# Low halves of every second gate and query tile by an adding DMA transfer; six query tiles from plain fp32 to three split products

## The chip, the cores and the metric

The kernel runs on one core of a Trainium2 chip. The metric is the device time of one execution in microseconds (us). TensorE (PE) multiplies, VectorE (DVE), ScalarE (ACT) and GpSimd (POOL) work on tiles in SBUF, and SyncE (SP) issues most of the DMA transfers; GpSimd issues a few on a queue of its own. Each engine runs its instructions in the order in which they are written and waits on semaphores.

## The reference

One inference step of a one-layer trunk for 256 prompt and 32 sample tokens, so 288 columns, with a model width of 2048. What matters here is its beginning: an RMS norm, one combined input projection, and its three uses.

```python
xn = rmsnorm(h, norm_mix_g)
proj = xn @ w_in                       # 2048 -> 2*1024 (conv) + 1024 (q) + 256 (k) + 256 (v)
a = proj[..., :2 * D_CONV]
glu = a[..., :D_CONV] * jax.nn.sigmoid(a[..., D_CONV:])
xin = concatenate([hist, glu]); y = depthwise_conv(xin, dw_w, width 31)   # then layer norm, silu
new_conv = xin[:, -(CONV_WIDTH - 1):]  # an output: the last 30 columns
q, k = partial_rope(...), partial_rope(...)
h = h + concatenate([conv_out, sliding_window_attention(q, k, v)]) @ w_out
h = h + cross_attention(rmsnorm(h), mem_k, mem_v)     # mem_k, mem_v from mem_prompt
h = h + peer_ffn(rmsnorm(h))                          # 16384 experts, product keys
```

The outputs are compared in fp32.

## The kernel before

**Layout.** Activations lie transposed, 128 rows of the width on the partitions and the 288 tokens as columns. A weight tile is 128 output rows by the whole width: `raw[:, s]`, 128 x 2048 fp32, 1 MB, from DRAM. Four of them (`RAW = 4`) are in SBUF; SyncE loads tile n once tile n - 4 is used (`slot_used`). The first 28 tiles of `w_mix` are the input projection: 16 **gate tiles** (0 to 15, in pairs: even ones give the gate, odd ones the value; 8 pairs for 8 channel tiles), then 12 **query tiles** (16 to 27: four for v and k, eight for q).

**Split products.** TensorE takes fp32 in a plain, slow form, or as fp32r in a fast form with fewer bits. A gate tile is made exact enough by splitting: ScalarE copies `raw` to a high half `wh` (L558), VectorE subtracts, `wl = raw - wh` (L955), and TensorE adds wh x xh, wh x xl and wl x xh for each of the 16 blocks (L1622 to L1624), so 48 matmuls of 288 columns. Both halves are made two tiles ahead (`AHEAD = 2`). The query tiles are not split: 16 plain fp32 matmuls `raw` x `xg` each (L1689). The trace has each of them as two records.

**VectorE between the tiles.** It multiplies the gate (L1037), then the value (L1043, L1044) into `glu`, moves query tiles out of PSUM (L1060, L1063) with the rotary embedding of earlier ones (`VKQ_TURN`, `VKQ_ROPE`: which tile is followed by which rotation), and works through the convolution: 8 channel tiles of 32 steps each (31 taps and a closing step, L1013, L1015, L1003, L1004). How many steps follow each tile is a table: `GLU_CONV` for the gate tiles, `VKQ_CONV` for the query tiles. ScalarE takes the sigmoid of a gate (L596); GpSimd multiplies it by the norm's factor (L2057).

**Memory operands.** After tile 19's load SyncE issues `memT` (4 x 0.5 MB) and `memr` (2 x 1 MB), which ScalarE scales (L607) and squares (L611), and then goes on with tiles 20 to 27. There `memr` and `memT` lie over `wh`, which the query tiles don't use. GpSimd writes out `new_conv` (L2061, L2062), zeroes `kz` and adds up `y` for the layer norm (L2070) as VectorE finishes channel tiles.

## Time and profile before

| | us |
|---|---|
| median of 3 runs | 1980.35 (1979.26 to 1983.44) |
| profiled execution | 1978.63 |
| its span in the trace | 1976.5 |
| gate tiles (from the start) | 0 to 128.3 |
| query tiles | 128.3 to 225 |
| attention with the memory tiles | 225 to 330 |
| the rest: output, cross attention, experts | 330 to 1976.5 |

Times in the rows are us from the span's start. In a timeline the square bracket is how long the engine had been idle before the instruction and what ended that. Matmul records overlap (they are pipelined), so the spacing of their starts tells what one costs, not their length.

### The profile page before, as it was taken

The page shows a single profiled execution, that of the slowest core. Times are in us where ns is not written, and L with a number is a line of the kernel's source. Part 1 is how long each engine was busy: PE and PEld are TensorE (multiplying, and loading weights), DVE is VectorE, ACT ScalarE, POOL GpSimd, SP SyncE. Part 2 cuts the span into 40 slices and gives each one's busy share as a digit, 9 for nine tenths or more (in the row PEclk, how much of TensorE's full clock was granted, in tenths as well). Part 3 has the DMA queues.
Part 4 walks back from the last instruction along what each step waited for, and adds up shares of the span by engine and source line. Part 5 has one row for each costly group of instructions (what it writes and reads, how often), then busy time and mean ns, then how long its engine had stood idle before and what let it go on. Part 6 is the DMA issues. An engine that isn't in the chain of part 4 may idle for free.

```text
span 1976.5 us, 29279 instructions
## 1 busy us (share of the span) xinstructions
PE 1941.4 (98%) x11100; PEld 1743.2 (88%) x11100; DVE 1534.6 (78%) x2297; ACT 857.9 (43%) x869; POOL 701.7 (36%) x497
## 2 busy tenths in 40 slices
PE   6999999999999999999999999999999999999998
PEld 6997888999999999999999999988888888888886
DVE  5999865566788898898888996677777767777776
ACT  4241145445435545555454545534433343344333
POOL 2010110221346778888767872010100011212310
PEclk9999999999999999999999999999999999999999
DMA  5465594444445788878778998899888999999984
GB/s 207 160 198 186 176 397 168 170 150 145 137 147 189 249 290 284 293 269 287 276 282 278 330 336 298 291 337 354 324 338 326 348 334 353 361 341 354 373 317 142
DMA packets 102523, 533.39 MB, mean 270 GB/s; under 512 B 20448, under 2 KB 22656, under 8 KB 46832
## 3 DMA queue, kind: packets, MB, share of 16 engines
q1 hardware_dynamic: 72880, 411.15, 58.0%
q0 software_dynamic: 24272, 106.33, 14.8%
q10 hardware_dynamic: 5296, 14.98, 1.9%
q8 instruction: 39, 0.64, 0.1%
q14 instruction: 36, 0.29, 0.0%
HBM read 493.53 MB, written 38.14 MB: 269 GB/s over the span
## 4 chain that ended last, share of the span: by engine, by line
PE 91%; DVE 4%; ACT 2%; DMA 1%; issue 1%; POOL 0%; DVEq 0%; SPq 0%; ACTq 0%; POOLq 0%
PE acc L1645 20%; PE mis L2024 17%; PE acc L2024 17%; PE acc L1646 10%; PE acc L1622 5%; PE acc L1624 5%; PE acc L1623 5%; PE acc L1689 5%; PE acc L1766 2%; DVE wl L955 1%; DMA raw<-in_u 1%; ACT wh L558 1%; PE mis L1746 1%; DVE xhl L963 0%; DMA hT<-in_xT 0%
## 5 line engine op out<-in xcount | busy, mean ns | idle before, releaser
L955 DVE TENSOR_TENSOR wl<-raw,wh 128x2048 fp32r<-128x2048 f32 x310 | 711.9, 2298 | 273.0 <-ACT wh L558 272.5
L558 ACT ACTIVATE wh<-raw 128x2048 fp32r<-128x2048 f32 x310 | 593.1, 1915 | 578.7 <-DMA raw<-in_v 410.3
L1645 PE MATMUL acc<-xhl,wh 128*128 128x448 f32 x2048 | 643.4, 375 | 1.6 <-DVE wl L955 1.6
L1646 PE MATMUL acc<-xhl,wl 128*128 128x224 f32 x2048 | 540.7, 264 | 0.0
L1645 PEld LDWEIGHTS acc<-xhl,wh 128*128 128x128 f32 x2048 | 384.1, 188 | 32.5 <-DVE wl L955 3.0
L1646 PEld LDWEIGHTS acc<-xhl,wl 128*128 128x128 f32 x2048 | 390.7, 191 | 0.0
L2185 POOL DMA_INDIRECT G<-gsum,cell x224 | 347.8, 1553 | 79.3 <-issue 67.4
L1622 PE MATMUL acc<-xhl,wh 128*128 128x288 f32 x736 | 220.4, 299 | 15.7 <-DVE wl L991 14.1
L1623 PE MATMUL acc<-xhl,wh 128*128 128x288 f32 x736 | 217.7, 296 | 0.0
L1624 PE MATMUL acc<-xhl,wl 128*128 128x288 f32 x736 | 217.4, 295 | 0.0
L2141 POOL DMA_INDIRECT ring<-in_ur,eidx x32 | 38.9, 1214 | 333.5 <-DVE hs L1450 321.5
L1622 PEld LDWEIGHTS acc<-xhl,wh 128*128 128x128 f32 x736 | 139.2, 189 | 18.1 <-DVE wl L991 14.1
L2141 POOL DMA_INDIRECT ring<-in_vr,eidx x32 | 66.7, 2085 | 227.6 <-DVE xrow L1538 193.4
L1623 PEld LDWEIGHTS acc<-xhl,wh 128*128 128x128 f32 x736 | 140.3, 191 | 0.1
L1624 PEld LDWEIGHTS acc<-xhl,wl 128*128 128x128 f32 x736 | 140.1, 190 | 0.0
L2024 PE MATMUL mis<-wh,ah 128*128 128x512 f32 x508 | 136.0, 389 | 0.0
L2024 PE MATMUL mis<-wh,al 128*128 128x512 f32 x508 | 135.8, 389 | 0.0
L2024 PE MATMUL mis<-wl,ah 128*128 128x512 f32 x508 | 135.8, 389 | 0.0
L2024 PE MATMUL acc<-wh,al 128*128 128x512 f32 x508 | 135.8, 389 | 0.0
L2024 PE MATMUL acc<-wh,ah 128*128 128x512 f32 x508 | 135.8, 389 | 0.0
L2024 PE MATMUL acc<-wl,ah 128*128 128x512 f32 x508 | 135.8, 389 | 0.0
L1015 DVE SCALAR_TENSOR_TENSOR cacc<-glu,par,cacc 128x318 f32<-128x318 f32 x232 | 113.2, 558 | 0.7 <-DVE gsb L1037 0.6
(337 smaller groups left out, 2617.5 us busy)
## 6 DMA issues: line engine op xcount, KB each, us to landing
raw<-in_u SPq DMA_DIRECT2D x128, 1024.0 KB, 5.7
raw<-in_v SPq DMA_DIRECT2D x128, 1024.0 KB, 5.9
raw<-in_w_mix SPq DMA_DIRECT2D x28, 1024.0 KB, 5.0
G<-zero SPq DMA_DIRECT2D x16, 1024.0 KB, 14.4
raw<-in_w_out SPq DMA_DIRECT2D x16, 1024.0 KB, 4.9
raw<-in_w_pq SPq DMA_DIRECT2D x16, 1024.0 KB, 4.9
gin<-G SPq DMA_DIRECT2D x32, 512.0 KB, 8.5
h<-hbg ACTq DMA_DIRECT2D x32, 448.0 KB
```

The lines of the kernel that those rows point to most:

```text
L558: act.activation(wh[:, n % 4], raw[:, n % 4], ACT.Copy).then_inc(hi_done, 1)
L955: dve.tensor_tensor(wl[:, n % 4], raw[:, n % 4], wh[:, n % 4].bitcast(F32), ALU.subtract).then_inc(lo_done, 1)
L1015: own.done(dve.scalar_tensor_tensor(cacc[:, a, :], x, w, cacc[:, a, :], ALU.mult, ALU.add))
L1622: pe.matmul(out, wh[:, wr, b, :], mh(j), start=(j == 0), stop=False)
L1623: pe.matmul(out, wh[:, wr, b, :], ml(j), start=False, stop=False)
L1624: ins = pe.matmul(out, wl[:, wr, b, :], mh(j), start=False, stop=(j == n - 1))
L1645: pe.matmul(acc[:, s, 0:2 * NU], wh[:, s, j, :], xu[:, j, 0:2 * NU], start=(j == 0), stop=False)
L1646: ins = pe.matmul(acc[:, s, 0:NU], wl[:, s, j, :], xuh[:, j, :], start=False, stop=(j == DT - 1))
L1689: ins = pe.matmul(acc[:, n % 4, 0:N], raw[:, n % 4, j, :], xg[:, j, :], start=(j == 0), stop=(j == DT - 1))
L2024: ins = pe.matmul(banks[t][c], ap[:, r, j, tok], w[:, s % 4, 4 * c:4 * c + 4, :].rearrange("p a n -> p (a n)"), start=False, stop=False)
L2141: pool.indirect_dma_start(ring[:, g % 2, :], None, dr["ur" if g < PICKS else "vr"], bass.IndirectOffsetOnAxis(ap=eidx[:, k:k + 1], axis=0) ...
L2185: pool.indirect_dma_start(cells_of, to, gsum[:, t, h, r:r + 1], None).then_inc(scattered[t], 16)
```

## The change

1. **Twelve tiles get `wl` another way** (`SUMMED`: 5, 7, ..., 27). ScalarE copies `raw` to `wh` as before and then writes the negated `raw` rounded the same way into `wl` (`high`). GpSimd then issues a DMA transfer that adds the same weight tile from DRAM to `wl` (`add_raw`, `accum_op=ALU.add`), so that `wl` holds raw - wh. VectorE does nothing for these tiles.
2. **TensorE does these tiles in another order** (`sum_slot`): for all blocks wh x xh and wh x xl, then a wait for the transfer (`sum_in`), then the 16 matmuls wl x xh.
3. **Six query tiles** (17, 19, ..., 27) become such tiles instead of plain fp32 ones. Their high halves use `wh` slots 0 and 1 alone (`high_slot`), and `memr` moves to other memory. ScalarE makes their halves for 17 and 19 at the end of the gate tiles, those for 21 to 27 behind `memr`'s squares.
4. **The convolution** is dealt otherwise: 148 steps in the gate tiles (112 before), 108 in the query tiles (144 before).
5. **The writes of `new_conv`** move from GpSimd to SyncE, ahead of `memT`, and wait there for tile 15's result (`acc_free`). GpSimd's additions of `y` stand between its transfers (`POOL_SUMS`).

```diff
 TURN_BANKS = 3
-GLU_CONV = (0, 0, 4, 8, 9, 9, 9, 9, 8, 8, 8, 8, 8, 8, 8, 8)
-VKQ_CONV = (14, 13, 15, 14, 15, 12, 14, 12, 13, 12, 4, 6)
+GLU_CONV = (0, 0, 4, 13, 8, 13, 8, 13, 8, 13, 8, 13, 8, 13, 13, 13)
+VKQ_CONV = (12, 9, 12, 9, 12, 8, 12, 8, 11, 8, 3, 4)
+SUMMED = (5, 7, 9, 11, 13, 15, 17, 19, 21, 23, 25, 27)
+POOL_SUMS = {19: (1, 2, 3), 21: (4,), 23: (5,), 25: (6,)}
...
         with ExitStack() as o:
-            memr, memT = sb(o, "memr", [P, 2, D]), sb(o, "memT", [P, DT, MEM])
+            sb(o, "over_wh", [P, 2 * DT * P])
+            memT = sb(o, "memT", [P, DT, MEM])
...
         with e:
+            with ExitStack() as o:
+                memr = sb(o, "memr", [P, 2, D])
...
+        def high_slot(n):
+            return n % 4 if n < VKQ0 else n // 2 % 2
+        def high_count(n):
+            return n + 1 if n < VKQ0 else VKQ0 + 1 + (n - VKQ0) // 2
...
             sp.wait_ge(slot_used, VKQ0)
+            sp.wait_ge(acc_free, VKQ0 + 4)
+            sp.wait_ge(hist_zero, 1)
+            sp.wait_ge(hist_in, 16)
+            sp.dma_start(dr["nconv_p"], glu[:, :, NP_:NP_ + HIST]).then_inc(nconv_out, 16)
+            sp.dma_start(dr["nconv_s"], glu[:, :, XW - HIST:XW]).then_inc(nconv_out, 16)
...
+            def high(n):
+                act.wait_ge(raw_in[n % 4], 16 * (n // 4 + 1))
+                act.activation(wh[:, high_slot(n)], raw[:, n % 4], ACT.Copy).then_inc(hi_done, 1)
+                if n in SUMMED:
+                    act.activation(wl[:, n % 4], raw[:, n % 4], ACT.Copy, scale=-1.0).then_inc(neg_done, 1)
                 for s in range(4):
-                    if not (last and s >= 4 - AHEAD):
-                        hi_next(GLU0, i, s)
+                    if not (last and s == 2):
+                        high(4 * i + s + AHEAD)
...
             glu_iteration(0, True)
-            with act.Fori(1, 3) as i:
-                glu_iteration(i)
-            glu_iteration(3, last=True)
-            act.wait_ge(lo_done, VKQ0)
-            act.sem_inc(hi_done, OUT0 - VKQ0)
+            for i in range(1, 4):
+                glu_iteration(i, last=i == 3)
+            high(VKQ0 + 3)
...
                 act.activation(memr[:, n], memr[:, n], ACT.Square, accum_out=gsp[:, n:n + 1]).then_inc(mem_sq, 1)
+            for n in range(VKQ0 + 5, MEM0, 2):
+                high(n)
...
                                mis[0:ln, bank, at:at + 256 * nt].rearrange("p (t c) -> p t c", t=nt), ACT.Copy).then_inc(vt_out, 1)
+            act.sem_inc(hi_done, OUT0 - high_count(MEM0 - 1))
...
                 for s in range(4):
-                    if not (last and s >= 4 - AHEAD):
+                    if 4 * i + s + AHEAD in SUMMED:
+                        dve.sem_inc(lo_done, 1)
+                    elif not (last and s >= 4 - AHEAD):
...
                 glu_iteration(i, last=i == 3)
-            dve.sem_inc(lo_done, OUT0 - VKQ0)
+            dve.sem_inc(lo_done, OUT0 - VKQ0 - 1)
...
                 slot(GLU0, 0, s, xh, xl)
-            with pe.Fori(1, 4) as i:
-                for s in range(4):
-                    slot(GLU0, i, s, xh, xl)
+            def sum_slot(n):
+                s, h = n % 4, high_slot(n)
+                pe.wait_ge(hi_done, high_count(n))
+                pe.wait_ge(acc_free, n + 1)
+                for j in range(DT):
+                    pe.matmul(acc[:, s, 0:N], wh[:, h, j, :], xh[:, j, :], start=(j == 0), stop=False)
+                    pe.matmul(acc[:, s, 0:N], wh[:, h, j, :], xl[:, j, :], start=False, stop=False)
+                pe.wait_ge(sum_in[s], 16 * (n // 4))
+                for j in range(DT):
+                    ins = pe.matmul(acc[:, s, 0:N], wl[:, s, j, :], xh[:, j, :], start=False, stop=(j == DT - 1))
+                ins.then_inc(slot_used, 1)
+            for n in range(4, VKQ0):
+                if n in SUMMED:
+                    sum_slot(n)
+                else:
+                    slot(GLU0, n // 4, n % 4, xh, xl)
...
             for n in range(12):
-                pe.wait_ge(raw_in[n % 4], 16 * (VKQ0 // 4 + n // 4 + 1))
-                pe.wait_ge(acc_free, VKQ0 + n + 1)
-                for j in range(DT):
-                    if n == 0 and j % 4 == 0:
-                        pe.wait_ge(xg_ready, j + 4)
-                    ins = pe.matmul(acc[:, n % 4, 0:N], raw[:, n % 4, j, :], xg[:, j, :], start=(j == 0), stop=(j == DT - 1))
-                ins.then_inc(slot_used, 1)
+                if VKQ0 + n in SUMMED:
+                    sum_slot(VKQ0 + n)
+                else:
+                    pe.wait_ge(raw_in[n % 4], 16 * (VKQ0 // 4 + n // 4 + 1))
+                    pe.wait_ge(acc_free, VKQ0 + n + 1)
+                    for j in range(DT):
+                        if n == 0 and j % 4 == 0:
+                            pe.wait_ge(xg_ready, j + 4)
+                        ins = pe.matmul(acc[:, n % 4, 0:N], raw[:, n % 4, j, :], xg[:, j, :], start=(j == 0), stop=(j == DT - 1))
+                    ins.then_inc(slot_used, 1)
...
                 pool.tensor_tensor(sqb[:, n % 2], src, src, ALU.mult).then_inc(sq_done, 1)
-            with pool.Fori(0, 4) as i:
-                for s in range(2):
-                    n = 2 * i + s
-                    pool.wait_ge(sig_done, n + 1)
-                    pool.wait_ge(acc_free, GLU0 + 4 + 2 * n)
-                    if s == 0:
-                        pool.wait_ge(rstd_done, 1)
-                    pool.tensor_tensor(gsb[:, 2, :], gsb[:, 1, :], rstd[:, 1, :], ALU.mult).then_inc(sgr_done, 1)
-            pool.wait_ge(acc_free, VKQ0 + 4)
-            pool.wait_ge(hist_zero, 1)
-            pool.wait_ge(hist_in, 16)
-            pool.dma_start(dr["nconv_p"], glu[:, :, NP_:NP_ + HIST]).then_inc(nconv_out, 16)
-            pool.dma_start(dr["nconv_s"], glu[:, :, XW - HIST:XW]).then_inc(nconv_out, 16)
-            pool.wait_ge(nconv_out, 32)
-            pool.wait_ge(conv_dve, 3)
-            pool.memset(kz[:], 0.0).then_inc(kz_zero, 1)
-            for t in range(1, CT - 1):
-                pool.wait_ge(conv_dve, t + 1)
-                if t > 1:
-                    own.wait(0)
-                own.done(pool.tensor_tensor(sqsum[:], y[:, 0, :] if t == 1 else sqsum[:], y[:, t, :], ALU.add))
+            def add_raw(n):
+                pool.wait_ge(neg_done, SUMMED.index(n) + 1)
+                pool.dma_start(wl[:, n % 4], dr["w_mix"][n], accum_op=ALU.add).then_inc(sum_in[n % 4], 16)
+            for n in range(8):
+                pool.wait_ge(sig_done, n + 1)
+                pool.wait_ge(acc_free, GLU0 + 4 + 2 * n)
+                if n == 0:
+                    pool.wait_ge(rstd_done, 1)
+                pool.tensor_tensor(gsb[:, 2, :], gsb[:, 1, :], rstd[:, 1, :], ALU.mult).then_inc(sgr_done, 1)
+                if 2 * n + 3 in SUMMED:
+                    add_raw(2 * n + 3)
+            for n in SUMMED:
+                if n <= VKQ0 + 1:
+                    continue
+                add_raw(n)
+                if n == VKQ0 + 3:
+                    pool.wait_ge(nconv_out, 32)
+                    pool.wait_ge(conv_dve, 3)
+                    pool.memset(kz[:], 0.0).then_inc(kz_zero, 1)
+                for t in POOL_SUMS.get(n, ()):
+                    pool.wait_ge(conv_dve, t + 1)
+                    if t > 1:
+                        own.wait(0)
+                    own.done(pool.tensor_tensor(sqsum[:], y[:, 0, :] if t == 1 else sqsum[:], y[:, t, :], ALU.add))
```

**ScalarE, from the high half of tile 14 on.** In `high`, L607 is the high half (`wh`) and L609 the negated copy (`wl`); `xg` is the plain operand of the query tiles; `gsb` is the sigmoid. Before:

```order
L590 ACTIVATE xg<-hT,par 128x288 x4
L596 ACTIVATE gsb<-gsb 128x288 [waits gate_done]
L558 ACTIVATE wh<-raw 128x2048 [waits raw_in3]
L590 ACTIVATE xg<-hT,par 128x288 x8
L596 ACTIVATE gsb<-gsb 128x288 [waits gate_done]
L590 ACTIVATE xg<-hT,par 128x288 x4
L607 ACTIVATE memT<-memT,par 128x256 [waits lo_done,mem_in0]
L607 ACTIVATE memT<-memT,par 128x256 x3
```

After:

```order
L617 ACTIVATE xg<-hT,par 128x288 x4
L623 ACTIVATE gsb<-gsb 128x288 [waits gate_done]
L607 ACTIVATE wh<-raw 128x2048 [waits raw_in3]
L609 ACTIVATE wl<-raw 128x2048
L617 ACTIVATE xg<-hT,par 128x288 x8
L623 ACTIVATE gsb<-gsb 128x288 [waits gate_done]
L607 ACTIVATE wh<-raw 128x2048 [waits raw_in1]
L609 ACTIVATE wl<-raw 128x2048
L617 ACTIVATE xg<-hT,par 128x288 x4
L607 ACTIVATE wh<-raw 128x2048 [waits raw_in3]
L609 ACTIVATE wl<-raw 128x2048
L632 ACTIVATE memT<-memT,par 128x256 [waits mem_in0]
```

The copies for tiles 15, 17 and 19 stand ahead of the last parts of `xg` and of `memT`, and tiles 21 on come behind `memr`.

**GpSimd, at the end of the gate tiles and in the query tiles.** Before:

```order
L2057 TENSOR_TENSOR gsb<-gsb,rstd 128x288 [waits acc_free]
L2050 REGISTER_ALU
L2050 COMPARE_AND_BRANCH
L2061 DMA out_nconv_p<-glu 1024x1x30 [waits hist_in,hist_zero,acc_free]
L2062 DMA out_nconv_s<-glu 1024x1x30
L2065 MEMSET glu 128x1024 [waits conv_dve,nconv_out]
L2070 TENSOR_TENSOR sqsum<-y 128x288 [waits conv_dve]
L2070 TENSOR_TENSOR sqsum<-sqsum,y 128x288 [waits pool_own,conv_dve] x5
L2072 DMA ckT<-in_ckT 128x256 [waits slot_used]
```

After:

```order
L2102 DMA wl<-in_w_mix 128x2048 [waits neg_done]
L2109 TENSOR_TENSOR gsb<-gsb,rstd 128x288 [waits acc_free,sig_done]
L2102 DMA wl<-in_w_mix 128x2048 [waits neg_done] x2
L2119 MEMSET glu 128x1024 [waits conv_dve,nconv_out]
L2124 TENSOR_TENSOR sqsum<-y 128x288 [waits conv_dve]
L2124 TENSOR_TENSOR sqsum<-sqsum,y 128x288 [waits pool_own,conv_dve] x2
L2102 DMA wl<-in_w_mix 128x2048 [waits neg_done]
L2124 TENSOR_TENSOR sqsum<-sqsum,y 128x288 [waits pool_own,conv_dve]
L2102 DMA wl<-in_w_mix 128x2048 [waits neg_done]
L2124 TENSOR_TENSOR sqsum<-sqsum,y 128x288 [waits pool_own,conv_dve]
```

Each adding transfer (`wl<-in_w_mix`) waits for its negated copy; the writes of `nconv` are gone from here, and the additions of `y` stand behind transfers.

**SyncE, from the last raw tile before the memory operands on.** Before:

```order
L462 DMA raw<-in_w_mix 128x2048
L458 REGISTER_ALU
L458 COMPARE_AND_BRANCH
L467 DMA memT<-in_memT 128x1024 [waits slot_used]
L467 DMA memT<-in_memT 128x1024 x3
L469 DMA memr<-in_mem_rows 128x2048 x2
L458 UNCONDITIONAL_BRANCH
L458 ISA
L462 ISA [waits slot_used]
L462 DMA raw<-in_w_mix 128x2048
```

After:

```order
L477 DMA raw<-in_w_mix 128x2048
L473 REGISTER_ALU
L473 COMPARE_AND_BRANCH
L484 DMA out_nconv_p<-glu 1024x1x30 [waits hist_zero,hist_in,acc_free,slot_used]
L485 DMA out_nconv_s<-glu 1024x1x30
L487 DMA memT<-in_memT 128x1024 x4
L489 DMA memr<-in_mem_rows 128x2048 x2
L473 UNCONDITIONAL_BRANCH
L473 ISA
L477 ISA [waits slot_used]
L477 DMA raw<-in_w_mix 128x2048
```

`memT` and `memr` now stand behind the two writes of `new_conv`, and these behind a wait for VectorE.

## Rows read from the trace of the kernel before

**Rows 1.** The page: busy time by engine, and the chain that ended last.

```profile
PE 1941.4 (98%) x11100; PEld 1743.2 (88%) x11100; DVE 1534.6 (78%) x2297; ACT 857.9 (43%) x869; POOL 701.7 (36%) x497
...
PE 91%; DVE 4%; ACT 2%; DMA 1%; issue 1%; POOL 0%; DVEq 0%; SPq 0%; ACTq 0%; POOLq 0%
```

**Rows 2.** Busy time by stage: gate tiles, then query tiles.

```profile
core 0: us, PE busy (x) PEld busy (x) DVE busy (x) ACT busy (x) POOL busy (x), PEclk, DMA share, GB/s
0.00:128.30 128.30, 113.34 (x800) 109.96 (x801) 103.08 (x166) 51.10 (x60) 17.38 (x21) 1.00 0.52 181
128.30:225.00 96.70, 96.70 (x409) 76.17 (x408) 88.67 (x210) 13.30 (x24) 7.81 (x9) 1.00 0.55 177
```

**Rows 3.** Timeline, ends of tiles: DVE after tiles 3, 16, 20; PE's first plain matmul.

```profile
52.36 0.42 DVE L1043 TENSOR_TENSOR glu<-acc,gsb 128x256 f32<-128x256 f32 x1 [0.17 <-PE acc L1624]
...
128.32 37.99 PE L1689 MATMUL acc<-xg,raw 128*128 128x288 f32 x156
...
136.35 0.46 DVE L1060 TENSOR_TENSOR kvT<-acc,rstd 128x288 f32<-128x288 f32 x1 [2.09 <-PE acc L1689]
...
167.32 0.42 DVE L1063 TENSOR_TENSOR qch<-acc,rstd 128x256 f32<-128x256 f32 x1 [0.22 <-PE acc L1689]
```

**Rows 4.** Timeline of DVE: low halves 14, 15, gate 14, value 15, convolution.

```profile
111.88 2.27 DVE L955 TENSOR_TENSOR wl<-raw,wh 128x2048 fp32r<-128x2048 f32 x1
...
118.94 2.28 DVE L955 TENSOR_TENSOR wl<-raw,wh 128x2048 fp32r<-128x2048 f32 x1
...
125.47 0.45 DVE L1037 TENSOR_TENSOR gsb<-acc,rstd 128x288 f32<-128x288 f32 x1
...
130.08 0.41 DVE L1043 TENSOR_TENSOR glu<-acc,gsb 128x256 f32<-128x256 f32 x1
...
184.23 6.53 DVE L1015 SCALAR_TENSOR_TENSOR cacc<-glu,par,cacc 128x318 f32<-128x318 f32 x14
```

**Rows 5.** Timeline of ScalarE: high half 5 behind its load, and a sigmoid.

```profile
50.88 1.92 ACT L558 ACTIVATE wh<-raw 128x2048 fp32r<-128x2048 f32 x1 [1.02 <-DMA raw<-in_w_mix]
...
114.56 0.45 ACT L596 ACTIVATE gsb<-gsb 128x288 f32<-128x288 f32 x1 [7.36 <-DVE gsb L1037]
```

**Rows 6.** DMA issues to 300 us: count, size, median us from issue to landing.

```profile
raw<-in_w_mix SPq DMA_DIRECT2D x28, 1024.0 KB, 5.0
G<-zero SPq DMA_DIRECT2D x16, 1024.0 KB, 14.4
...
out_nkv_p<-kvT POOLq DMA_DIRECT2D x1, 256.0 KB, 3.1
```

**Rows 7.** Busy time by stretch, as rows 2; the last two figures are DMA share and GB/s.

```profile
78.00:90.00 12.00, 12.00 (x93) 12.00 (x93) 11.84 (x19) 2.32 (x4) 1.13 (x1) 1.00 0.53 175
...
138.00:140.00 2.00, 2.00 (x10) 1.56 (x9) 2.00 (x6) 0.58 (x2) 0.00 (x0) 1.00 1.07 79
...
150.00:152.00 2.00, 2.00 (x10) 1.58 (x9) 2.00 (x5) 1.55 (x2) 0.00 (x0) 1.00 1.01 426
```

**Rows 8.** Timeline: DMA issues of SyncE around 130 us.

```profile
128.66 0.33 SPq L462 DMA_DIRECT2D raw<-in_w_mix  x1
129.20 1.99 SPq L467 DMA_DIRECT2D memT<-in_memT  x4
...
136.42 23.61 SPq L462 DMA_DIRECT2D raw<-in_w_mix  x4
```

**Rows 9.** Landing times of the raw tiles issued at 136 and at 144 us.

```profile
DMA to landing us min/median/max: 18.1/18.1/18.1
...
DMA to landing us min/median/max: 12.8/12.8/12.8
```

**Rows 10.** Timeline of PE: its first matmuls after the idle start.

```profile
14.10 0.61 PE L1622 MATMUL acc<-xhl,wh 128*128 128x288 f32 x1 [14.10 <-DVE wl L991]
...
14.98 0.45 PE L1622 MATMUL acc<-xhl,wh 128*128 128x288 f32 x1
15.22 0.45 PE L1623 MATMUL acc<-xhl,wh 128*128 128x288 f32 x1
```

More of the change, by code:

```diff
@@ L352, in build @@
         memr_in = [sem(f"memr_in{n}") for n in range(2)]
+        neg_done = sem("neg_done")
+        sum_in = {n: sem(f"sum_in{n}") for n in (1, 3)}
         raw_in = [sem(f"raw_in{n}") for n in range(RAW)]
```

## The prediction, made before the changed kernel was run

> **What bounds the kernel now.** The page's header and its chain of waits come first: TensorE is busy 98% of the span and holds 91% of the chain [rows 1]. So a change pays only if it takes time off TensorE, or costs if it makes TensorE wait. The change works in the first 225 us; the table by stage shows TensorE without a gap in the twelve query tiles (96.70 of 96.70 us), while DVE has 88.67 us of work there and ScalarE only 13.30 [rows 2].
>
> Then the length of one tile. In the DVE timeline an instruction that waited for PE marks a tile's end. Gate tile 3 ends at 52.36 and the first plain fp32 matmul starts at 128.32, twelve split tiles later: 75.96/12 = **6.33 us for a split tile**. The ends of query tiles 16 and 20 are at 136.35 and 167.32, with four plain tiles between: 30.97/4 = **7.74 us for a plain tile** [rows 3]. (I number tiles 0 to 15 gate, 16 to 27 query.)
>
> **What the change takes off TensorE.** Six query tiles go from one plain fp32 product to three split products: 6 x (7.74 - 6.33) = **8.5 us**, all on the path. The rotations that follow five of the tiles stay. In the gate tiles TensorE does the same 48 matmuls in another order (low half last), at no price. Each stall below is subtracted from 8.5.
>
> **DVE in the gate tiles.** It loses six low halves of 2.28 us and gets 36 more convolution steps (148 instead of 112; 14 take 6.53 us, 0.47 each, about 0.48 with a channel's ends). It is already the late one: the gate product of tile 14 starts at 125.47, though TensorE ended that tile at 128.32 - 6.33 = 122.0, and the low half of tile 15 ends at 121.2, 0.8 us before TensorE wants it [rows 3, 4]. Up to the low half of tile 14 there are 21 more steps (+10.0 us) and five low halves less (each adds about 2.22 back to back). The first of these buys nothing, since DVE then waits for tile 3's end at 52.36, so -8.9. Tile 14's low half is therefore ready at 114.1 + 1.1 = 115.2, and is wanted at 115.6: it fits by 0.4 us. No stall; if it is missed, a bound of 1 us. Tile 15's result is read later than now: 130.08 + 31 x 0.48 - 5 x 2.22 = 133.9. In the query tiles DVE has 36 steps less (-17 us) against 8.5 us less time, so it isn't the bound.
>
> **ScalarE and the adding transfer in the gate tiles.** An odd tile's low half is now: gate product of the tile three earlier, sigmoid 0.44, high half 1.9, negated copy 1.9 (both as the high half of [rows 5]), the issue on GpSimd, the transfer, then TensorE's last third. The transfer for tile 15 is issued at 115.2 + 0.45 + 0.45 + 3.75 = 119.9; TensorE needs it 2/3 into the tile, at 122.0 + 4.2 = 126.2. So **6.3 us are there**. For tile 5 they are 8.2, since its raw tile is in at 50.88 [rows 5].
>
> The trace of before has no adding transfer. Low bound: it moves the same 1 MB from the same tensor as a raw load. At 426 GB/s, the rate in 150 to 152 [rows 7], 1 MB (1.049 million bytes) takes 2.46 us, and a small GpSimd issue took 3.1 us to land with 256 KB (0.6 us of data), so 2.5 us fixed [rows 6]: **5.0 us**. Twice the data time, if reading the target costs as much as reading the source: **7.4 us**. High bound, however far: the 14.4 us that 1 MB of zeros took to land [rows 6]. The low end needs no new wait; 7.4 us makes one of 1.1 us, 14.4 us one of 8 us and more. I take 5.0, since the raw load is the nearest row: same bytes, same rows, same engines, and the second operand lies in SBUF.
>
> The Trainium skill speaks against this (Collectives: The Full Stack, "Why ReduceScatter is half of AllGather"): an inline add is slow because it takes two source reads on one ring, so it runs at half the rate of a copy. By that rule the price is 7.4 us and the result is the first rival's; no row of this trace shows it.
>
> **The query tiles: the transfers collide.** Here I expect what part of the gain is lost. Now SyncE issues raw tile 19 at 128.66, memT and memr (4 MB) from 129.20, raw tile 20 at 136.42 [rows 8]. The DMA engines are busy all the while, but at 138 to 140 they move only 79 GB/s at a share of 1.07: GpSimd's two history writes go out in small pieces there [rows 7]. Raw tile 20 lands after 18.1 us, at 154.5; raw tile 21, issued at 144, after 12.8, at 156.8 [rows 9]. TensorE starts tile 20 at 128.3 + 4 x 7.74 = 159.3: 4.8 us spare. Three things now eat that:
> - tile 20 is wanted earlier, at 128.3 + 2 x 7.74 + 2 x 6.33 = 156.4;
> - the history writes stand on SyncE's queue ahead of memT and wait for tile 15's result (133.9), so the queue holds nothing but raw tile 19 until about 134.8 (two issues and the start behind the wait), where now memT follows raw tile 19 at once, at about 132.5: +2.3 us;
> - the transfers of tiles 17 (issued about 131.3) and 19 (about 140) share the engines: the first fills the gap before 134.8, the second adds 2.5 us.
>
> Raw tile 20 lands at 154.5 + 2.3 + 2.5 = 159.3: **a stall of 2.9 us**. Tile 21's low half comes after it: raw at 161.6, two ScalarE copies to 165.4, transfer to 170.4; wanted at 159.3 + 7.74 + 0.5 + 4.2 = 171.7. No more stall. memr's squares come before it on ScalarE (twice 1.9 us behind memr's landing, some 2.5 us before raw tile 20), in time. Tiles 23, 25 and 27 have their raw tile three tiles ahead, some 16 us of room. Tile 17's transfer has 140.3 - 131.3 = 9 us, tile 19's 14.
>
> Sum: -8.5 + 2.9 = -5.6 us. The profiled execution took 1978.63 us (span 1976.5), 1.7 below the median of 1980.35; the difference is put on the median: **1974.8 us**. What follows the query tiles starts that much earlier and is unchanged.
>
> **Rivals.**
> *The add runs at half the rate (7.4 us).* Each of the two transfers beside the memory loads costs 4.9 us of engine time, and the first is only half done at 134.8: raw tile 20 lands at 154.5 + 2.3 + 2.6 + 4.9 = 164.3, raw tile 21 at 166.6, its negated copy is ready at 170.4, the sum at 177.8, against 156.4 + 8.2 + 4.2 = 168.8 wanted without any stall. Stalls 9.0 in all: **1980.9**. For it: an add needs two operands. Against: no row has shown the engines bound by reading.
> *No stall at all:* the history writes cost less behind each other than among others (four fifths of the rate are lost at 138 to 140). Then **1971.9**.
> *Slower: the loop of gate and add paces the gate tiles.* Place: tiles 5 to 15. It decides from 6.3 us per transfer. At 12 us, tile 15 would wait 5.7 us by the single sum, and the loop itself (0.9 + 4.6 + 12 + 2.1 = 19.6 us from the end of tile 2n to that of 2n+3, against 19.0 now) adds 1 to 3 us; with the later query tiles, whose wait for tile 21 grows to 9.0 + 4.6, the stalls come to about 14 to 18: **1986 to 1990**. At 14.4 us it is past 1995. For it: 1 MB was seen to take 14.4 us; raw loads, one per 6.33 us, share the engines. Against: the engines are only 0.5 busy in the gate tiles [rows 2, 7].
> *The clock.* After 14.1 us without work TensorE's first matmuls came every 0.24 us [rows 10] instead of the 0.13 of a split tile (6.33/48), the lower of its two levels. One tile's 48 at that spacing would cost 5 us more; the first tile was through with it after about half. The granted clock is 1.00 in all stretches. A stall of 3 us may or may not bring that; I count up to 3 us in the range.
>
> **How the numbers follow.** Forecast 0.42 (own range 1971.5 to 1978), half-rate add 0.25 (1978 to 1984), no stall 0.08, slower loop 0.23, anything else 0.02. A measurement here tells 0.2%, 4 us, from no change: faster is below 1976.4, slower above 1984.3. Faster: most of the forecast and no stall, 0.47. Within: nearly all of the half-rate case and the forecast's upper edge, 0.27. Slower: the loop and a little of the half rate, 0.26. Range 1970.5 to 1990, which leaves out the loop's upper half.
>
> **What would show it.** Landing of the wl transfers: 5, 7.4 or over 10 us. PE's waits: none in the gate tiles, one of about 3 us before the first matmul of tile 20 (plain fp32, released by the raw load); a wait in a query tile's last third, behind the wl transfer, means the half-rate case; waits at tiles 11 to 15 the loop. The query stage should last 128.3 to about 219. I am wrong if a gate tile's plain low half is late (DVE), or if the adding transfer is not near a raw load.

## The result: slower by 0.33%, where the query tiles gained nothing and the gate tiles lost 5.8 us

The changed kernel takes **1985.84 us** (median of 8 runs, 1984.72 to 1989.94) against 1980.44 (8 runs, 1978.24 to 1983.44) for the kernel before in the same comparison: a ratio of 1.0033, interval 1.0025 to 1.0042 (the two medians alone give 1.0027). The forecast was 1974.8, 5.6 us faster; it is 5.4 us slower. The profiled execution took 1985.61 us, of which 1983.4 are span.

The page of the changed kernel, busy time and chain (answering [rows 1]):

```profile
PE 1936.9 (98%) x11196; PEld 1745.8 (88%) x11196; DVE 1518.0 (77%) x2291; ACT 890.7 (45%) x887; POOL 733.7 (37%) x507
...
PE 81%; DVE 8%; DMA 5%; ACT 2%; issue 2%; SPq 1%; POOL 0%; DVEq 0%; ACTq 0%; POOLq 0%
```

TensorE has 4.5 us less work in a span 6.9 us longer, and DMA has gone from 1% of the chain to 5%. The page does not say where; the timeline of TensorE does (a first plain matmul starts the query stage, the first transposition of kvT ends it; answering [rows 3]):

```profile
134.10 7.92 PE L1738 MATMUL acc<-xg,raw 128*128 128x288 f32 x32
...
168.09 10.16 PE L1738 MATMUL acc<-xg,raw 128*128 128x288 f32 x32 [5.33 <-DMA raw<-in_w_mix]
...
230.55 1.25 PE L1754 MATMUL mis<-cst,kvT 128*96 128x128 f32 x10
```

The gate tiles end at 134.10 instead of 128.32. The query stage takes 96.45 us, as before (224.99 - 128.32 = 96.67), though it holds 8.5 us less matrix work. So there are two losses: 5.8 us in the gate tiles, 8.3 us in the query tiles. What TensorE waited for up to 330 us (us in total, times, longest):

```profile
PE acc L1738 <- DMA raw<-in_w_mix: 5.3, 1, 5.3
PE acc L1702 <- DMA wl<-in_w_mix: 4.4, 6, 1.1
```

The twelve adding transfers, from issue to landing:

```profile
DMA to landing us min/median/max: 8.3/11.1/13.8
```

The six sums of the gate tiles are each late by a little (1.1 us at most); raw tile 20 is late once, by 5.3 us. After that wait tile 20 takes 10.16 us and not 7.92. Why, the table by stretch shows (the figure before the last two is the granted clock):

```profile
160.00:164.00 4.00, 2.76 (x19) 2.30 (x18) 3.36 (x8) 2.62 (x5) 0.00 (x0) 1.00 1.01 427
164.00:168.00 4.00, 0.00 (x0) 0.00 (x0) 3.39 (x8) 3.10 (x4) 0.00 (x0) 0.70 1.01 426
168.00:172.00 4.00, 3.91 (x8) 2.87 (x9) 0.00 (x0) 1.45 (x1) 0.00 (x0) 0.50 1.03 428
172.00:176.00 4.00, 4.00 (x17) 3.10 (x16) 0.00 (x0) 2.26 (x2) 1.45 (x2) 0.95 0.52 211
```

The idle stretch drops the grant to 0.50, its lower level (1.2 of 2.4 GHz), until about 172. The query stage's 8.3 us are 5.3 of wait, 2.2 of lower clock, and 0.8 of small things. SyncE's timeline (answering [rows 8]) shows why raw tile 20 is late:

```profile
135.12 0.60 SPq L484 DMA_DIRECT2D out_nconv_p<-glu  x1
135.77 2.69 SPq L485 DMA_DIRECT2D out_nconv_s<-glu  x1
138.50 7.60 SPq L487 DMA_DIRECT2D memT<-in_memT  x4
146.14 3.55 SPq L489 DMA_DIRECT2D memr<-in_mem_rows  x2
150.05 6.60 SPq L477 DMA_DIRECT2D raw<-in_w_mix  x3
```

SyncE does not only start late, it issues slowly: 7.60 us for the four memT issues against 1.99, and 3.55 for memr's two against 1.01. Raw tile 20 could have been issued when tile 16 was done, at 142.0; it is issued at 150.05 and lands 17.99 us later.

Last, the DMA queues between 50 and 215 us (packets, MB, share of 16 engines' time): before, changed.

```profile
q0 software_dynamic: 96, 0.25, 1.4%
```

```profile
q0 software_dynamic: 1616, 11.80, 37.6%
```

The last sum lands after 215, so 11.80 MB are eleven and a quarter sums of 1.049 MB. 37.6% of 165 us over 11.25 sums is **5.5 us of all sixteen engines for each sum**, where 1 MB at 426 GB/s [rows 7] takes 2.46. (Two of the expectations below say 5.2, the same share divided by twelve.) The six sums of e6_gate_only and the six of e7_spread give 5.5 to 5.6 as well (6.29 MB each, 20.2% and 20.1%).

### The profile page after: what moved, and what is told of

Its sections match the earlier page's. It is cut to its first block, busy times and chain, and to the rows that moved or that the text cites. A ratio compares the mean times of both kernels' runs of the same rounds, so it can differ in the third digit from the quotient of the medians.

```text
span 1983.4 us, 29448 instructions
## 1 busy us (share of the span) xinstructions
PE 1936.9 (98%) x11196; PEld 1745.8 (88%) x11196; DVE 1518.0 (77%) x2291; ACT 890.7 (45%) x887; POOL 733.7 (37%) x507
## 4 chain that ended last, share of the span: by engine, by line
PE 81%; DVE 8%; DMA 5%; ACT 2%; issue 2%; SPq 1%; POOL 0%; DVEq 0%; ACTq 0%; POOLq 0%
PE mis L2073 17%; PE acc L2073 17%; PE acc L1675 17%; PE acc L1676 8%; PE acc L1652 4%; PE acc L1654 4%; PE acc L1653 4%; DVE wl L983 3%; PE acc L1815 2%; PE acc L1738 2%; DMA wl<-in_w_mix 2%; DMA raw<-in_u 2%; ACT wh L578 1%; DMA raw<-in_w_mix 1%; PE acc L1702 1%
## 5 line engine op out<-in xcount | busy, mean ns | idle before, releaser
L983 DVE TENSOR_TENSOR wl<-raw,wh 128x2048 fp32r<-128x2048 f32 x304 | 697.7, 2297 | 277.7 <-ACT wh L578 265.4
L578 ACT ACTIVATE wh<-raw 128x2048 fp32r<-128x2048 f32 x296 | 566.2, 1915 | 561.7 <-DMA raw<-in_v 411.2
L1675 PEld LDWEIGHTS acc<-xhl,wh 128*128 128x128 f32 x2048 | 384.1, 188 | 34.0 <-DVE wl L983 4.5
L1676 PEld LDWEIGHTS acc<-xhl,wl 128*128 128x128 f32 x2048 | 390.8, 191 | 0.0
L2239 POOL DMA_INDIRECT G<-gsum,cell x224 | 353.4, 1578 | 79.2 <-issue 68.0
L1652 PE MATMUL acc<-xhl,wh 128*128 128x288 f32 x640 | 191.6, 299 | 16.2 <-DVE wl L1019 14.6
L1653 PE MATMUL acc<-xhl,wh 128*128 128x288 f32 x640 | 189.2, 296 | 0.0
L1654 PE MATMUL acc<-xhl,wl 128*128 128x288 f32 x640 | 188.8, 295 | 0.0
L2195 POOL DMA_INDIRECT ring<-in_vr,eidx x32 | 79.8, 2495 | 216.9 <-DVE xrow L1568 182.1
L1652 PEld LDWEIGHTS acc<-xhl,wh 128*128 128x128 f32 x640 | 120.8, 189 | 18.5 <-DVE wl L1019 14.6
L1653 PEld LDWEIGHTS acc<-xhl,wh 128*128 128x128 f32 x640 | 121.8, 190 | 0.1
L1654 PEld LDWEIGHTS acc<-xhl,wl 128*128 128x128 f32 x640 | 121.6, 190 | 0.0
```

Source lines behind the costliest of these rows:

```text
L578: act.activation(wh[:, n % 4], raw[:, n % 4], ACT.Copy).then_inc(hi_done, 1)
L983: dve.tensor_tensor(wl[:, n % 4], raw[:, n % 4], wh[:, n % 4].bitcast(F32), ALU.subtract).then_inc(lo_done, 1)
L1652: pe.matmul(out, wh[:, wr, b, :], mh(j), start=(j == 0), stop=False)
L1653: pe.matmul(out, wh[:, wr, b, :], ml(j), start=False, stop=False)
L1654: ins = pe.matmul(out, wl[:, wr, b, :], mh(j), start=False, stop=(j == n - 1))
L1675: pe.matmul(acc[:, s, 0:2 * NU], wh[:, s, j, :], xu[:, j, 0:2 * NU], start=(j == 0), stop=False)
```

## The theory and its rivals

**Theory.** (a) The addition itself makes the transfer about twice as costly for the engines and as late as 11 us. In the gate tiles this closes a loop: gate product, sigmoid, two copies, sum, last third of the tile three later, value product, next gate product. The sums are issued at 51.63 and 65.48, 13.85 us apart, where two split tiles take 12.66. VectorE's own work lies in that loop too: between value and gate product it does convolution steps and a low half, so it reaches the gate product of tile 8 only at 88.39, 2.5 us after TensorE went on to tile 9 (85.91):

```profile
85.91 0.29 PE L1698 MATMUL acc<-xhl,wh 128*128 128x288 f32 x1
...
86.19 2.29 DVE L983 TENSOR_TENSOR wl<-raw,wh 128x2048 fp32r<-128x2048 f32 x1
88.39 0.45 DVE L1067 TENSOR_TENSOR gsb<-acc,rstd 128x288 f32<-128x288 f32 x1
```

(b) In the query tiles it is the crowd at tiles 16 to 21: the sums, 4 MB of memory loads, and the history writes whose place on SyncE's queue holds the issues behind them.

**Rivals.** A second stream beside the raw loads is slow whatever it does (against a). The crowd slows SyncE's issues, not the writes ahead of them (against b). One loss causes the other. The DMA engines can't carry the sums in any arrangement. VectorE, with 36 more convolution steps in the gate tiles, is late by itself (against a).

All eleven experiments, by the two rows shown above (first plain matmul, first transposition), their profiled executions:

| kernel | query stage starts | ends | length | median us | ratio to before, interval |
|---|---|---|---|---|---|
| before | 128.32 | 224.99 | 96.67 | 1978.2 to 1980.4 | |
| changed | 134.10 | 230.55 | 96.45 | 1985.84 | 1.0033 (1.0025 to 1.0042) |
| e1_hist_late | 136.68 | 231.94 | 95.26 | 1983.9 | 1.0037 (1.0027 to 1.0047) |
| e2_early | 130.37 | 228.67 | 98.30 | 1983.84 | 1.0030 (1.0017 to 1.0042) |
| e3_early_late | 131.88 | 231.25 | 99.37 | 1982.14 | 1.0018 (1.0009 to 1.0028) |
| e4_query_only | 127.38 | 225.20 | 97.82 | 1980.89 | 1.0010 (1.0000 to 1.0019) |
| e5_plain_copy | 127.22 | 217.81 | 90.59 | 1972.93 | one run |
| e6_gate_only | 134.33 | 231.00 | 96.67 | 1983.48 | 1.0031 (1.0021 to 1.0041) |
| e7_spread | 127.85 | 217.89 | 90.04 | 1974.74 | 0.9981 (0.9971 to 0.9990) |
| e8_spread_g2 | 127.66 | 219.07 | 91.41 | 1974.43 | 0.9978 (0.9969 to 0.9988) |
| e9_hist_pool | 134.35 | 231.91 | 97.56 | 1987.92 | 1.0041 (1.0027 to 1.0055) |
| e10_spread_full | 131.43 | 226.79 | 95.36 | 1979.14 | 1.0001 (0.9987 to 1.0015) |
| e11_two_halves | 127.65 | 221.20 | 93.55 | 1978.22 | 0.9998 (0.9988 to 1.0007) |

The span left after the query stage, where the code is the same in all, is 1749.6 to 1755.6 us in the profiled executions, so a median follows the stage's end only to a few us. I read causes from the stage and gains from the ratios. A stage time is of one execution: the gate tiles of the changed kernel, e1 and e9 are the same code and end at 134.10 to 136.68, those with no sum in them (before, e4, e7, e11) at 127.38 to 128.32.

## Experiments on the addition

**e5_plain_copy.** The same transfers without the addition. It leaves out the subtraction, so its products are not those of the reference; only its time is of use.

```diff
-pool.dma_start(wl[:, n % 4], dr["w_mix"][n], accum_op=ALU.add).then_inc(sum_in[n % 4], 16)
+pool.dma_start(wl[:, n % 4], dr["w_mix"][n]).then_inc(sum_in[n % 4], 16)
```

> The twelve adding transfers become plain transfers of the same bytes from the same queue to the same buffers at the same places (so wl holds the weights and not their low halves, and the third product of the summed tiles is wrong); everything else is the changed kernel's. Theory (the adding itself is what is slow, about twice the time of all sixteen DMA engines for a byte): the landings of wl fall from 11.1 us to 5 to 7, tiles 5 to 15 end at 128 to 129 instead of 134.1, the DMA share of the gate tiles falls back, and the time is 1974 to 1979. Rival (it is the second stream beside the raw loads, or GpSimd's queue, whatever the transfer does with its bytes): landings of 9 us and more, gate tiles end after 132, 1983 to 1987. In both SyncE's issues behind the history writes stay slow (memT x4 over 5 us) if the writes are their cause.

Measured 1972.93. Landing times, then the software queue between 50 and 215 us, then TensorE's one wait for a transfer up to 330 us:

```profile
DMA to landing us min/median/max: 5.1/6.1/12.1
```

```profile
q0 software_dynamic: 1728, 12.58, 21.8%
```

```profile
PE acc L1738 <- DMA raw<-in_w_mix: 2.1, 1, 2.1
```

The twelve transfers of 1 MB land after 6.1 us instead of 11.1 and take 21.8% of 165 us / 12 = 3.0 us of the engines instead of 5.5. The gate tiles end at 127.22, at no loss, and the query stage gains 6.1 us. The rival (any second stream is slow) is out, and so is VectorE as a cause by itself, since its steps are the same: the query stage ends 12.7 us earlier than in the changed kernel (217.81 against 230.55), and the two differ in that one operand alone. memT's four issues take 3.89 us here, down from 7.60 and under the 5 us that I expected with the writes ahead: the writes are not the whole of that.

**e11_two_halves.** e7_spread (below) with each sum in two transfers.

```diff
+for h in (slice(0, DT // 2), slice(DT // 2, DT)):
+    pool.dma_start(wl[:, n % 4, h], dr["w_mix"][n][:, h], accum_op=ALU.add).then_inc(sum_in[n % 4], 16)
-pe.wait_ge(sum_in[s], 16 * sum(m <= n and m % 4 == s for m in SUMMED))
+pe.wait_ge(sum_in[s], 32 * sum(m <= n and m % 4 == s for m in SUMMED))
```

> e7_spread with each sum as two adding transfers of 512 KB, one behind the other on GpSimd's queue; TensorE waits for both. Theory (the price goes by the byte, about 5.2 us of all sixteen DMA engines for 1 MB, over a fixed part of 2 to 3 us): the first half lands after 5 to 6.5 us, the median of all halves is 6 to 9, and the time is within 2 us of e7_spread (1973 to 1977). Rival (the price is mostly fixed per transfer): both halves take 8 us and more, the second lands after 14 to 16, sums are late, 1978 to 1984.

Measured 1978.22, about 3.5 us worse than e7_spread, compared over two sets of runs. Landing times of the two halves of tile 17, and of tile 27's first half, issued into the quietest stretch (DMA share 0.39 between 203 and 206); then, of e7_spread, tile 23's whole transfer, the quickest there (share 0.65 between 176 and 180):

```profile
DMA to landing us min/median/max: 6.2/8.5/10.8
...
DMA to landing us min/median/max: 5.7/5.7/5.7
```

```profile
DMA to landing us min/median/max: 8.3/8.3/8.3
```

At best 512 KB land after 5.7 us here and 1 MB after 8.3 in e7_spread: 2.6 us for a half, so an estimate of 5.2 us per MB over 3.1 fixed, near the 5.5 that the engines' share gives. The two stretches were not equally busy, so the split is rough. And the second half of tile 17 lands 10.8 us after an issue 1.1 us later, where the whole took 8.7 in e7_spread: the median of all halves is 10.5, above the 6 to 9 expected. The time is outside the theory's range and at the lower end of the rival's, so neither holds whole: a lone half is quicker, a pair of halves is not.

## Experiments on the two losses

**e6_gate_only** sums tiles 5 to 15 only, **e4_query_only** tiles 17 to 27 only (with the convolution shares of before).

```diff
-SUMMED = (5, 7, 9, 11, 13, 15, 17, 19, 21, 23, 25, 27)
+SUMMED = (5, 7, 9, 11, 13, 15)
...
+SUMMED = (17, 19, 21, 23, 25, 27)
```

> Only tiles 5 to 15 get a sum; all query tiles stay plain fp32, with the changed kernel's convolution shares and its order on SyncE. Theory (two separate losses): gate tiles end near 134 again (+5.8), the query stage keeps its 96.6 us or a little more (raw tile 20 late behind the memory loads, 0 to 5 us), so 1986 to 1991. Rival (the gate tiles are slowed by what the query stage asks of ScalarE, GpSimd and the DMA engines): gate tiles end before 130, under 1983.

> Only the six query tiles get the adding transfer; the gate tiles have their low halves from VectorE again, and the convolution is dealt as in the kernel before (112 and 144 steps). History writes on SyncE ahead of memT as in the changed kernel. My theory: the gate tiles end at 128.3 again; the history writes are issued at about 131.2 instead of 134.9, so raw tile 20 lands near 164, wanted at 156.4: a wait of about 8 us and 2.5 us of half clock, against 8.5 gained: about 1982, range 1980 to 1984. Rival (the wait at tile 20 comes from VectorE's lateness alone): about 1976. VectorE with 144 steps in the shorter query tiles may add up to 3 us at their end.

e6 measured 1983.48: the query stage starts at 134.33 and takes 96.67 us. The whole gate loss is there without any sum in the query tiles, and a query stage of plain tiles loses nothing on top (the wait at tile 20 is gone; the median is 2.5 us under the expected range). e4 measured 1980.89, as expected: no loss in the gate tiles (127.38), and a query stage longer than before (97.82 against 96.67), in a profiled execution that came out 2.5 us above the median. Its SyncE and TensorE rows:

```profile
131.20 7.88 SPq L487 DMA_DIRECT2D memT<-in_memT  x4
139.12 2.70 SPq L489 DMA_DIRECT2D memr<-in_mem_rows  x2
142.18 31.44 SPq L477 DMA_DIRECT2D raw<-in_w_mix  x5
...
162.57 10.55 PE L1738 MATMUL acc<-xg,raw 128*128 128x288 f32 x32 [6.78 <-DMA raw<-in_w_mix]
```

Again 7.88 us for memT's issues, raw tile 20 late by 6.78, a tile of 10.55 us. So each loss is there without the other.

**e2_early: the gate loop alone.** ScalarE's copies of an odd gate tile and the adding transfer go one step earlier, ahead of the even tile's sigmoid.

```diff
 for n in range(8):
+    if 2 * n + 3 in SUMMED:
+        add_raw(2 * n + 3)
     pool.wait_ge(sig_done, n + 1)
 ...
-    if 2 * n + 3 in SUMMED:
-        add_raw(2 * n + 3)
```

> The changed kernel with ScalarE's two copies for each odd gate tile (and 17) made one step earlier, before the sigmoid of the gate instead of behind it, and GpSimd's transfer issued ahead of its gate product. This gives each adding transfer some 5 us more before TensorE wants it. My theory: the gate tiles lose 5.8 us (they end at 134.1 instead of 128.3) because the transfer takes 11.5 us and only 6 to 8 are there; they then end at 128.5 to 129.5 again. But the history writes still wait for VectorE, so raw tile 20 lands no earlier than about 165 and the wait before it grows by what the gate tiles gave back: 1983 to 1986 in all. Rival: VectorE, with 36 more convolution steps, is what makes the gate tiles late; then they still end near 134. Second rival: the two losses are independent, and the time falls to 1980.

1983.84, in the expected range. The query stage starts at 130.37, 3.7 us earlier than in the changed kernel, though not at the expected 128.5 to 129.5. The loop through the gate product is opened and most of the gate loss goes; two sums are still late, by 2.2 us together. What came free was lost again: tile 20 still waits for its raw tile (5.25 us, then 10.42 us for the tile), and the sum of tile 19 waits 1.85.

**e1_hist_late: the writes off SyncE's queue until raw tile 23 is issued. e9_hist_pool: the writes back on GpSimd's queue.**

```diff
-sp.dma_start(dr["nconv_p"], glu[:, :, NP_:NP_ + HIST]).then_inc(nconv_out, 16)
-sp.dma_start(dr["nconv_s"], glu[:, :, XW - HIST:XW]).then_inc(nconv_out, 16)
 for n in range(4):
     sp.dma_start(memT[:, 4 * n:4 * n + 4, :], dr["memT"][:, 4 * n:4 * n + 4, :]).then_inc(mem_in[n], 16)
 for n in range(2):
     sp.dma_start(memr[:, n], dr["mem_rows"][:, n]).then_inc(memr_in[n], 16)
-stream("w_mix", GLU0, 5, 7)
+stream("w_mix", GLU0, 5, 6)
+sp.dma_start(dr["nconv_p"], glu[:, :, NP_:NP_ + HIST]).then_inc(nconv_out, 16)
+sp.dma_start(dr["nconv_s"], glu[:, :, XW - HIST:XW]).then_inc(nconv_out, 16)
+stream("w_mix", GLU0, 6, 7)
```

The diff is e1's, which also clears kz behind the sum of tile 25. In e9 the two writes stand on GpSimd's queue ahead of the sum of tile 19, and SyncE's order is otherwise the changed kernel's.

> The changed kernel with one move: SyncE issues the two writes of new_conv behind raw tile 23 instead of ahead of memT (and GpSimd clears kz behind the transfer of tile 25). My theory: in the changed kernel the writes ahead of memT wait for VectorE until 134.9 and then hold up SyncE's issues (memT 138.5 to 146.1, memr to 149.7, raw tile 20 only at 150.05), so raw tile 20 lands at 168, TensorE waits 5.3 us and then runs about 2.5 us late at half the clock. With the writes out of the way raw tile 20 lands before it is wanted (about 162), both go: 1985.8 - 5.3 - 2.5 = about 1978. The gate tiles stay as slow (end near 134). Rival: it is the adding transfers that fill the DMA engines; then raw tile 20 is still late and the time stays at 1984 to 1986.

> The changed kernel with the two history writes back on GpSimd's queue, ahead of add 19, and off SyncE's queue. Theory (the writes on SyncE's queue hold SyncE up: its memT issues took 7.6 us there and about 2.1 us in the two kernels that had the writes later): memT x4 issued in 2 to 3 us, raw tile 20 issued about 5 us earlier (near 145), TensorE's wait at tile 20 falls from 5.3 us to under 2, but a sum (19 or 21) is exposed by 1 to 4 us in its place; 1982 to 1985. Rival (the crowd of transfers slows SyncE's issues, not the writes): memT x4 still over 5 us, tile 20 still late by 5, 1985 to 1987.

SyncE's memT issues in e1, then in e9:

```profile
137.60 2.16 SPq L482 DMA_DIRECT2D memT<-in_memT  x4
```

```profile
135.22 2.89 SPq L482 DMA_DIRECT2D memT<-in_memT  x4
```

2.16 and 2.89 us instead of 7.60, and tile 20 no longer waits for its raw tile in either: without the writes ahead on the same queue the issues are quick. But the writes alone don't make 7.60 either. In e6, with the writes ahead of memT and no sum under way:

```profile
137.44 4.35 SPq L487 DMA_DIRECT2D memT<-in_memT  x4
```

It took the writes and the sums together to reach 5.88 (e2), 7.60 and 7.88 us (e4). But both kernels missed their times, 1983.9 and 1987.92. What is late next is the sum of tile 21 (and of tile 19 in e9). TensorE's rows of e1, then of e9:

```profile
182.87 3.83 PE L1703 MATMUL acc<-xhl,wl 128*128 128x288 f32 x16 [4.47 <-DMA wl<-in_w_mix]
```

```profile
162.84 3.74 PE L1697 MATMUL acc<-xhl,wl 128*128 128x288 f32 x16 [2.20 <-DMA wl<-in_w_mix]
...
182.67 3.21 PE L1697 MATMUL acc<-xhl,wl 128*128 128x288 f32 x16 [3.17 <-DMA wl<-in_w_mix]
```

The wait of 5.3 for a load had hidden these. In e1 the gate tiles also ended 2.6 us later than in the changed kernel, with the same code up to that point: its waits for sums come to 6.4 us there instead of 4.4, and one of them, 1.80 us at tile 15, was followed by the lower clock. Its gate sums landed no later (11.2 us on average in both); why more was waited for them stays open.

**e3_early_late** has both edits (e1's and e2's).

> Both moves together: copies and transfers of odd gate tiles one step earlier, history writes behind raw tile 23. My theory: both losses go and the 8.5 us of the six query tiles remain: 1980.4 - 8.5 = 1972, range 1971 to 1974, TensorE without a wait of over 0.5 us from tile 1 to 27. Rival, the DMA engines are overloaded by 12 MB more: waits of 2 us or more remain at raw tiles 20 or 21 and the time is 1976 or more. Rival, VectorE: the gate tiles end at 130 or later.

1982.14, far from the expected 1972. The memT issues take 2.03 us, tile 20 does not wait, but sums are late at tile 17 (3.25 us) and tile 21 (4.21), and the stage takes 99.37 us in the profiled execution, which came out 4 us above the median. So removing two named waits was not enough; that made the crowd itself the suspect. The gate tiles end at 131.88, against its rival's 130 or later: one sum is late there (1.98 us), with the lower clock behind it.

## Taking the crowd apart: a version that beats both

**e7_spread.** Sums in the query tiles only; the memory loads spread out. The rows memr are loaded behind raw tile 7 and squared in the gate tiles; memT comes in two pairs behind raw tiles 20 and 22; the history writes go behind raw tile 21, ScalarE's copies of tiles 19 and 21 ahead of memT's scaling. The convolution is dealt as before the change, and tile 17's copies and transfer come one step earlier, as in e2.

```diff
-stream("w_mix", GLU0, 1, 5)
...
-stream("w_mix", GLU0, 5, 7)
+stream("w_mix", GLU0, 1, 2)
+for n in range(2):
+    sp.dma_start(memr[:, n], dr["mem_rows"][:, n]).then_inc(memr_in[n], 16)
+stream("w_mix", GLU0, 2, 5)
+for n in range(VKQ0 + 4, MEM0):
+    sp.wait_ge(slot_used, n - 3)
+    sp.dma_start(raw[:, n % 4], dr["w_mix"][n]).then_inc(raw_in[n % 4], 16)
+    if n in (VKQ0 + 4, VKQ0 + 6):
+        for m in range(n - VKQ0 - 4, n - VKQ0 - 2):
+            sp.dma_start(memT[:, 4 * m:4 * m + 4, :], dr["memT"][:, 4 * m:4 * m + 4, :]).then_inc(mem_in[m], 16)
+    if n == VKQ0 + 5:
...
+        sp.dma_start(dr["nconv_p"], glu[:, :, NP_:NP_ + HIST]).then_inc(nconv_out, 16)
+        sp.dma_start(dr["nconv_s"], glu[:, :, XW - HIST:XW]).then_inc(nconv_out, 16)
```

> Sums only in query tiles 17 to 27; the gate tiles and the convolution as in the kernel before; the memory rows are loaded and squared in the gate tiles, memT comes in two pairs behind raw tiles 20 and 22, the history writes go behind raw tile 21, each summed tile's copies are ahead of memT's scaling. Theory (the sums are fine where DMA engines and ScalarE are free, the loss is the crowd at tiles 16 to 21): no wait of TensorE over 1 us before tile 23, the query stage 88 to 91 us, 1972 to 1976. Rival (the adding transfers alone keep the DMA engines busy, so that moving the rest does not help): a sum or a raw tile again late by over 4 us, with a stretch at the lower clock, 1979 to 1984.

1974.74 us, 0.9981 of before (0.9971 to 0.9990): faster than both kernels. e4 has the same six sums without the spreading and stands at 1.0010, so the moves are worth some 0.3%. TensorE's timeline, then its only wait for a sum:

```profile
127.85 7.92 PE L1757 MATMUL acc<-xg,raw 128*128 128x288 f32 x32
...
217.89 1.26 PE L1773 MATMUL mis<-cst,kvT 128*96 128x128 f32 x10
```

```profile
PE acc L1721 <- DMA wl<-in_w_mix: 1.2, 1, 1.2
```

The stage is 90.04 us, 6.6 less than before. The sums are no quicker than elsewhere (10.5 us median, 8.3 to 13.5), and the DMA engines are as busy (0.97 between 128 and 192): the transfers simply stand where 10 us are there. The second history write takes 5.65 us to issue here too (at 143.25), but TensorE does not wait for what stands behind it. The rival that the engines can't carry them is out for six sums.

**e8_spread_g2** also sums gate tiles 11 and 15, and moves ten convolution steps there.

```diff
-SUMMED = (17, 19, 21, 23, 25, 27)
+SUMMED = (11, 15, 17, 19, 21, 23, 25, 27)
```

> As e7_spread, and gate tiles 11 and 15 are summed too, their transfers issued ahead of the gate's multiplication, with ten steps of the convolution moved from the query tiles to the gate tiles. Theory: VectorE is the next limit of a query stage of 88 us (85 us of work in it), ten steps less of it there give 1 to 3 us against e7_spread, and two lone sums in the gate tiles have 15 us and more of room each and cost under 0.5: 1971 to 1975. Rival (any sum in the gate tiles delays them by about 1 us each, 5.8 for six): 2 us slower in the gate tiles, no better than e7_spread.

1974.43, the same as e7_spread. Two lone sums cost the gate tiles nothing (127.66); they landed after 8.5 and 7.9 us. Less VectorE work in the query tiles buys nothing that shows, against what I expected; TensorE waited 2.6 us for sums there (1.2 in e7_spread), which may hide a small gain.

**e10_spread_full**: the spreading and e2's early issue with all twelve sums and the changed kernel's convolution shares.

> All twelve sums of the changed kernel and its convolution shares, with the spread memory loads and late history writes of e7_spread and the gate tiles' adding transfers issued one step earlier (as in e2_early). Theory (two separate losses, that of the query tiles removed by the spreading, that of the gate tiles by the early issue up to the DMA engines' own limit): gate tiles end at 128 to 131, tile 16 is waited for by up to 2 us, query stage 89 to 92 us; 1975 to 1980, worse than e7_spread by 1 to 4 us. Rival (the DMA engines, about 5.2 us of all sixteen per sum, cannot carry twelve sums): sums late again in both stages, 1982 to 1986.

1979.14, level with before (interval 0.9987 to 1.0015), where the changed kernel is at 1.0033. The gate tiles end at 131.43 and the query stage takes 95.36 us, in a profiled execution 2.6 us above the median; 128 to 131 and 89 to 92 were expected. TensorE's wait for sums:

```profile
PE acc L1721 <- DMA wl<-in_w_mix: 5.6, 3, 3.3
```

One of the three is in the gate tiles (1.75 us at tile 9, whose last 16 matmuls then took 3.73 us at the lower clock instead of 2.38), two in the query tiles (0.57 us at tile 17, 3.33 at tile 21). So six sums close together in the gate tiles cost about 3 us even issued early, and they buy TensorE nothing, since gate tiles are split products either way. And with twelve sums the spreading does not clear the query tiles: for twelve, the rival that the engines can't carry them is not out.

## Why the prediction was wrong, step by step

- **What a tile costs** (6.33 split, 7.74 plain; 8.5 us for six): right. e7_spread's stage is 6.6 us shorter with 1.2 us of wait in it, e5's 6.1 with 2.1: 7.8 and 8.1.
- **The adding transfer at 5.0 us: this is the step that failed.** "The raw load is the nearest row: same bytes, same rows, same engines" was near for the copy (6.1 us in e5, beside the raw loads) and wrong for the addition: 8.3 at the least, 11.1 in the middle. With the copy at 6.1 us the kernel took 1972.93 (one run), near the forecast 1974.8, so nearly all of the miss hangs on this term. The half-rate rival's 7.4 us was near the quickest sum of all runs (7.8, in e2 and e4): its 4.9 us of engine time was measured as 5.5. By the Trainium skill's rule of half rate (Collectives: The Full Stack, "Why ReduceScatter is half of AllGather") the trace agrees roughly: 5.5 us of engine time is 2.2 times the 2.46 of the full rate, and 1.8 times the 3.0 of e5's copies. What neither said is what sharing adds. Of the six gate sums, the five that had two raw loads issued while they were under way landed after 11.3 to 11.8 us, the one with one (at 95.02) after 9.6, and the two of e8, with one each, after 8.5 and 7.9. An estimate from the engine times, 5.5 + 2 x 3.0 = 11.5 and 5.5 + 3.0 = 8.5, gives about that.
- **The slower rival**, the loop of gate and add, is what happened in the gate tiles. Its point of decision (6.3 us) and its price at 12 us were near: the sums came at 11.1 and the time at 1985.84, beside its 1986 to 1990. Its picture was rough: not one wait of 5.7 us at tile 15, but six of up to 1.1, as the period of two tiles grows from 12.66 to 13.85 us. Its loop was also too short outside the transfer: TensorE goes on from tile 4 at 58.16 and the sum of tile 7 is issued at 65.48, 7.3 us later instead of 5.5, since VectorE starts the gate product only at 60.64. That its total fits is in part luck: it had 1 to 3 us from the loop and 13.6 from the query tiles, where 5.8 and 8.3 were measured. "The engines are only 0.5 busy" was no argument against it: that was the mean before, and while a sum was under way the share went to 0.99 and 1.02 (58 to 64, 70 to 77).
- **VectorE fits by 0.4 us**: right. The changed kernel does not try it, since the late sums gave more room (tile 15's result was read at 134.3, forecast 133.9, a fit by chance). e5 does, with the same steps and no late sum: tile 14's low half is ready at 114.0, TensorE goes on to tile 14 at 114.51 and waits for nothing in the gate tiles, and tile 15's result is read at 132.44.
- **Raw tile 20 late** was right in kind (after the plain copy too, by 2.1 us) and mis-sized: a landing at 159.3 was forecast, it came at 168.04. Its issue slipped by 13.6 us (136.42 to 150.05). Some 5.7 of it are tile 16's later end; in the other 8 SyncE was still issuing memT and memr, 7.60 + 3.55 us against 1.99 + 1.01 before. My term held only two short issues and a start, none of that. From issue to landing nothing changed (17.99 us against 18.1 [rows 9]).
- **Tile 21: "no more stall"** held only because tile 20 waited. e1 and e3 show it late by 4.5 and 4.2, as the half-rate rival had it.
- **The clock**: "up to 3 us", and a stall of 5.3 us cost 2.2.

In place of -8.5 + 2.9 the sum is: -8.5 + 5.8 (gate loop) + 5.3 (raw tile 20) + 2.2 (clock) + 0.8 = +5.6, where the medians give +5.4. The 0.8 is what was left over, so the sum closes by its making. Two parts stay open: how much of the gate loss VectorE's extra steps bring once the sums are late (no run has six gate sums with fewer steps), and why SyncE's issues slow down.

## What to carry to other kernels

An adding transfer is not priced like a plain one: count its operand as well as its bytes, give 1 MB of it 10 us and more from issue to use beside other loads, and keep it out of a loop that its reader closes. Moving work to the DMA engines pays only where it takes time off the engine on the path: here six sums in the query tiles let TensorE use the shorter split products and give 4 us, and the other six take work from VectorE, which was not waited for, and cost the gate tiles 3 to 6. When one wait is taken away, look for the one it covered (raw tile 20, then the sums of 21, 19 and 17), and ask of a crowded stretch which of its transfers could simply stand elsewhere.
